# Order of the products in the up projections of a two-block transformer kernel, and the layout of their activation tile

## What is computed

```python
def swiglu(h, w_in, w_out):
    a, g = jnp.split(h @ w_in, 2, axis=-1)
    return (jax.nn.silu(a) * g) @ w_out
...
mlp = jnp.einsum('bsf,fd->bsd', jnp.square(jax.nn.relu(jnp.einsum('bsd,df->bsf', x, w_up[i]))), w_down[i])
gate = jax.nn.sigmoid((jnp.einsum('bsd,de->bse', x, w_ple_gate[i]) + b_ple_gate[i]).astype(jnp.float32)).astype(x.dtype)
```

## Time and profile before

| | |
|---|---|
| median of the three runs | 2022.68 us |
| lowest and highest run | 2021.26, 2022.79 us |
| span of the profiled execution | 2020.7 us |
| PE busy | 1988.9 us, 98% of the span |
| DVE, ACT busy | 1322.7 us, 857.5 us |
| mean granted TensorE clock | 0.997 |
| moved by DMA | 319.19 MB |

### The profile page before, as it was taken

One profiled execution on the slowest core, in us unless ns is written; L12 is line 12 of the kernel. 1 busy time (PEld: TensorE's weight loads), 2 busy tenths in 40 slices (PEclk: granted clock), 3 DMA queues, 4 the chain that ended last, 5 costly groups with the idle time before them and its releaser, 6 DMA issues.

```text
span 2020.7 us, 25508 instructions
## 1 busy us (share of the span) xinstructions
PE 1988.9 (98%) x10263; PEld 1654.0 (82%) x10263; DVE 1322.7 (65%) x1642; ACT 857.5 (42%) x1007; POOL 68.4 (3%) x121
## 2 busy tenths in 40 slices
PE   8999999999999999999999999999999999999998
PEld 5878778778888888877778888899888888988887
DVE  5886979556555354576776565766866577678565
ACT  5332332224322222446665554554544356445442
POOL 0000000010111000000000000000000000000000
PEclk9999999999999999999999999999999999999999
DMA  9544444252554343332137555545655554546552
GB/s 357 184 151 136 144 148 145 84 167 74 172 155 158 104 151 126 102 113 84 53 103 219 168 177 177 188 165 170 216 194 193 176 172 162 196 157 218 189 190 81
DMA packets 250759, 319.19 MB, mean 158 GB/s; under 512 B 10113, under 2 KB 166066, under 8 KB 250130
## 3 DMA queue, kind: packets, MB, share of 16 engines
q1 hardware_dynamic: 235152, 262.77, 40.2%
q0 software_dynamic: 14416, 53.14, 7.8%
q10 hardware_dynamic: 1074, 1.66, 0.2%
HBM read 316.48 MB, written 1.05 MB: 157 GB/s over the span
## 4 chain that ended last, share of the span: by engine, by line
PE 86%; DVE 6%; ACT 2%; DVEq 2%; DMA 1%; issue 1%; ACTq 1%; SPq 0%
PE ps L2326 14%; PE ps L2327 14%; PE ps L2321 8%; PE ps L2881 6%; PE ps L3142 6%; PE ps L2340 5%; PE ps L2336 5%; PE ps L2337 5%; PE ps L2798 3%; PE ps L2269 3%; PE ps L3145 3%; PE ps L2406 2%; PE ps L2887 2%; PE ps L2891 2%; PE ps L2888 2%; PE ps L2801 2%
## 5 line engine op out<-in xcount | busy, mean ns | idle before, releaser
L1241 DVE TENSOR_TENSOR w_lo<-raw,w_hi 128x2048 fp32r<-128x2048 f32 (+1 forms) x244 | 553.0, 2271 | 239.1 <-ACT w_hi L609 238.3
L609 ACT ACTIVATE w_hi<-raw 128x2048 fp32r<-128x2048 f32 (+1 forms) x244 | 462.0, 1897 | 254.3 <-PE ps L2321 149.6
L2326 PE MATMUL ps<-w_hi,big_hi 128*128 128x512 f32 x760 | 298.8, 393 | 0.9 <-DVE big_lo L1739 0.7
L2327 PE MATMUL ps<-w_hi,big_lo 128*128 128x512 f32 x760 | 296.2, 390 | 0.0
L2336 PE MATMUL ps<-hT_hi,w_hi 128*128 128x512 f32 (+1 forms) x512 | 192.4, 380 | 1.9 <-issue 1.0
L2337 PE MATMUL ps<-hT_lo,w_hi 128*128 128x512 f32 (+1 forms) x512 | 190.3, 376 | 0.0
L2326 PE MATMUL ps<-w_hi,hT_hi 128*128 128x512 f32 x416 | 167.7, 403 | 4.6 <-DVE hT_lo L1246 4.6
L2326 PEld LDWEIGHTS ps<-w_hi,big_hi 128*128 128x128 f32 x760 | 142.8, 188 | 30.4 <-issue 1.0
L2327 PEld LDWEIGHTS ps<-w_hi,big_lo 128*128 128x128 f32 x760 | 142.9, 188 | 28.9 <-issue 0.5
L2327 PE MATMUL ps<-w_hi,hT_lo 128*128 128x512 f32 x416 | 163.2, 392 | 0.0
L3142 PE MATMUL ps<-h_both,w_hi 128*128 128x512 f32 x512 | 128.0, 392 | 0.0
(11 more groups left out here) (314 smaller groups left out, 3027.4 us busy)
## 6 DMA issues: line engine op xcount, KB each, us to landing
raw<-ffn_w_in SPq DMA_DIRECT2D x88, 512.0 KB, 5.1
raw<-w_in SPq DMA_DIRECT2D x80, 512.0 KB, 4.6
raw<-w_up SPq DMA_DIRECT2D x64, 512.0 KB, 4.7
raw<-w_down SPq DMA_DIRECT2D x64, 512.0 KB, 4.5
raw<-ret_w_in SPq DMA_DIRECT2D x48, 512.0 KB, 5.4
front<-ada_w POOLq DMA_DIRECT2D x24, 1024.0 KB, 5.5
raw<-ffn_w_out SPq DMA_DIRECT2D x40, 512.0 KB, 4.5
raw<-ada_w POOLq DMA_DIRECT2D x64, 256.0 KB, 4.3
```

The costliest lines, as they stand in the source:

```text
L609: act.activation(SPLIT_HI[PAIR_OF[u]][:, 0:m], raw[:, RAW_OF[u], 0:m], ACT.Copy).then_inc(sem["hi_ready"], 1)
L1241: op(SPLIT_LO[PAIR_OF[u]][:, 0:m], raw[:, RAW_OF[u], 0:m], SPLIT_HI[PAIR_OF[u]][:, 0:m].bitcast(F32), ALU.subtract).then_inc(sem["lo_ready ...
L2326: pe.matmul(out, x[0][:, t * P:(t + 1) * P], w, start=start, stop=False)
L2327: pe.matmul(out, x[1][:, t * P:(t + 1) * P], w, start=False, stop=False)
```

## The change

The tile's axes are exchanged, so that the high and low columns of one k-tile lie side by side. The short products of a half no longer follow its long ones: those of half 0 stand one by one ahead of the long ones of half 1, and those of half 1 ahead of the long ones of half 0 of the next unit. The last half of each group of up units has its short ones in a run, as before. `used` of a unit moves to the last short product of its half 1, which now lies within the next unit, unless it is the group's last. The waits (`up_read`, `hi_ready`, `lo_ready`) stand where they stood, at the head of a unit and behind its first 8 long products. The lists of ACT, DVE, SP and POOL are not touched. Groups are units 2, 3 to 7, 8 to 11, 12 to 15 and 16 to 21 in the first block (`ups1`), and U0 to U3, four times two, and U12 to U15 in each layer (`ups`).

```diff
-        h2_both = sb("h2_both", [P, 2, KD, 256], F32R, hT_at)
-        h2_hi, h2_lo = (h2_both[:, j, :, :] for j in range(2))
+        h2_both = sb("h2_both", [P, KD, 2, 256], F32R, hT_at)
+        h2_hi, h2_lo = (h2_both[:, :, j, :] for j in range(2))
...
+                def up_low(n, j, k):
+                    out, js = up_out(n, j)
+                    w = SPLIT_LO[PAIR_OF[start_of[f"U{n}"]]].rearrange("p (k n) -> p k n", k=KD)
+                    return pe.matmul(out[:, 0, :], w[:, k, js], h2(k)[0], start=False, stop=(k == KD - 1))
+
+                def ups(first, last):
+
+                    for n in range(first, last):
+                        if n >= 2:
+                            pe.wait_ge(sem["up_read"], 20 + 16 * l + n - 1)
+                        w = unit(f"U{n}", 0, KD)
+                        out, js = up_out(n, 0)
                         for k in range(KD):
-                            pe.matmul(out, w[0][:, k, js], h2_both[:, :, k, :], start=(k == 0), stop=False)
+                            if n > first:
+                                m = up_low(n - 1, 1, k)
+                            pe.matmul(out, w[0][:, k, js], h2_both[:, k, :, :], start=(k == 0), stop=False)
+                        if n > first:
+                            used(m)
                         lows(w)
+                        out, js = up_out(n, 1)
                         for k in range(KD):
-                            i = pe.matmul(out[:, 0, :], w[1][:, k, js], h2(k)[0], start=False, stop=(k == KD - 1))
-                    used(i)
+                            up_low(n, 0, k)
+                            pe.matmul(out, w[0][:, k, js], h2_both[:, k, :, :], start=(k == 0), stop=False)
+                    for k in range(KD):
+                        m = up_low(last - 1, 1, k)
+                    used(m)
...
-                up(0)
-                up(1)
-                for g in range(5):
-                    up(2 * g + 2)
-                    up(2 * g + 3)
+                ups(0, 4)
+                down(0)
+                for g in range(1, 5):
+                    ups(2 * g + 2, 2 * g + 4)
                     down(g)
-                for n in range(12, 16):
-                    up(n)
+                ups(12, 16)
                 down(5)
```

More of the change, by code:

```diff
@@ L2787, in up1_rows, with up1_out, up1_low, ups1 @@
                 return m
[L2789 to L2796, removed]
-                    for k in range(KD):
-                        pe.matmul(out, w[0][:, k, js], h2_both[:, :, k, :], start=(k == 0), stop=False)
+            def up1_out(i, j):
+                return ps[:, UP_PAIR[(i + 1) % 2] + j, :].rearrange("p (a n) -> p a n", a=2), slice(j * P, (j + 1) * P)
+            def up1_low(i, j, k):
+                out, js = up1_out(i, j)
+                w = SPLIT_LO[PAIR_OF[FIRST_AT[f"f{i}"]]].rearrange("p (k n) -> p k n", k=KD)
+                return pe.matmul(out[:, 0, :], w[:, k, js], h2(k)[0], start=False, stop=(k == KD - 1))
+            def ups1(first, last):
+                for i in range(first, last):
+                    if i >= 4:
+                        pe.wait_ge(sem["up_read"], i - 3)
+                    elif i == 3:
+                        pe.wait_ge(sem["hid_lo"], 22 + 2)
+                    w = unit(f"f{i}", KD)
+                    out, js = up1_out(i, 0)
+                    for k in range(KD):
+                        if i > first:
+                            m = up1_low(i - 1, 1, k)
+                        pe.matmul(out, w[0][:, k, js], h2_both[:, k, :, :], start=(k == 0), stop=False)
+                    if i > first:
+                        used(m)
                     lows(f"f{i}")
+                    out, js = up1_out(i, 1)
                     for k in range(KD):
-                        m = pe.matmul(out[:, 0, :], w[1][:, k, js], h2(k)[0], start=False, stop=(k == KD - 1))
+                        up1_low(i, 0, k)
+                        pe.matmul(out, w[0][:, k, js], h2_both[:, k, :, :], start=(k == 0), stop=False)
+                for k in range(KD):
+                    m = up1_low(last - 1, 1, k)
                 used(m)
@@ L2824, in _ @@
             pe.wait_ge(sem["x_ready"], 12)
-            up1(2)
+            ups1(2, 3)
             for i in range(2):
@@ L2831, in _ @@
             gate_row(4)
-            up1(3)
-            for i in range(4, 8):
-                up1(i)
+            ups1(3, 8)
             pe.wait_ge(sem["rg_read"], 4)
             down1(0)
-            for i in range(8, 12):
-                up1(i)
+            ups1(8, 12)
             down1(1)
-            for i in range(12, 16):
-                up1(i)
+            ups1(12, 16)
             down1(2)
-            for i in range(16, 22):
-                up1(i)
+            ups1(16, 22)
             down1(3)
@@ L3132, in layer, with up_out @@
                     used(tile_rows(bank(4 + c), 1, w, h2, k0, 4, k0 == 0, k0 == 4))
[L3134 to L3140, removed]
-                        for k in range(KD):
-                            pe.matmul(out, w[0][:, k, js], h2_both[:, :, k, :], start=(k == 0), stop=False)
+                def up_out(n, j):
+                    return ps[:, UP_PAIR[n % 2] + j, :].rearrange("p (a n) -> p a n", a=2), slice(j * P, (j + 1) * P)
+                def up_low(n, j, k):
+                    out, js = up_out(n, j)
+                    w = SPLIT_LO[PAIR_OF[start_of[f"U{n}"]]].rearrange("p (k n) -> p k n", k=KD)
+                    return pe.matmul(out[:, 0, :], w[:, k, js], h2(k)[0], start=False, stop=(k == KD - 1))
+                def ups(first, last):
[4 more added lines that the diff above has]
+                        out, js = up_out(n, 0)
+                        for k in range(KD):
+                            if n > first:
+                                m = up_low(n - 1, 1, k)
+                            pe.matmul(out, w[0][:, k, js], h2_both[:, k, :, :], start=(k == 0), stop=False)
+                        if n > first:
+                            used(m)
                         lows(w)
+                        out, js = up_out(n, 1)
                         for k in range(KD):
-                            i = pe.matmul(out[:, 0, :], w[1][:, k, js], h2(k)[0], start=False, stop=(k == KD - 1))
-                    used(i)
+                            up_low(n, 0, k)
+                            pe.matmul(out, w[0][:, k, js], h2_both[:, k, :, :], start=(k == 0), stop=False)
+                    for k in range(KD):
+                        m = up_low(last - 1, 1, k)
+                    used(m)
                 def hid(k):
```

## The result

The changed kernel takes **2026.52 us** (median of 14 runs, 2025.11 to 2027.29); the kernel before, run beside it, 2022.36 us (14 runs, 2021.26 to 2022.79). The ratio is 1.0021, with an interval of [1.0013, 1.0028] that lies wholly above 1: slower by 0.2%, some 4 us. The time lies above the stated range, which ended at 2025.6. The profiled execution has a span of 2024.6 us, 3.9 more than before, at the same mean granted clock of 0.997.

What follows compares the result with a forecast made beforehand. PE's own back-to-back products, busy 98% of the span, were taken as the bound. Shorts taken apart, -4.15 us, and holes at the layer starts, +1.85, gave -2.3: 2022.7 to 2020.4 us, range 2017.6 to 2025.6.

Steps and rivals of the forecast that it cites:

- the price of the pair: Up units on PE: a single short and a long together cost 342 ns, 114 + 228, against 349.2 today.
- short products singly: Up units on PE: 87 runs of eight shorts taken apart, 72 of them counting, for -4.15 us.
- upper bound: Pair on PE: a short within a run, 120, and a long right behind one, 234, together 354 ns.
- lower bound: Pair on PE: a short right behind a long, 114, and an undisturbed long, 226.5, together 340.5 ns.
- The first rival: Pairs on PE: every switch costs, 348 to 354 ns a pair, kernel slower at 2024.0 to 2027.7 us; 25%.
- The layout: Activation tile: 512 adjacent columns for the long products' moving operand, put at 0.
- The holes: Start of each layer: PE waits 1.2 us ahead of U3 for DVE's add of U1; together +1.85 us.
- The second rival: Layer starts: the waits at U3 don't hold PE, 86 runs count, -5.0, 2017.7 us; 10%.
- The steady units: Units after the layer starts: `used` moves back, 1.4 us of slack left, 15 waits cost nothing.
- The third rival: Steady units: DVE reads too late everywhere, 15 holes of about 0.9, +13, 2034 us; 5%.
- The loads hidden all along: Pairs on PE: the pair stays at 349.2 ns and only holes of 2.1 remain, 2024.8 us; 7%.
- Queues, and all else: Queues and waits: same instructions, no transfer; splits and SP's loads some 1.7 us later, needed over 16 us after.

Runs made afterwards that it cites:

- experiment 11: Changed kernel with the gate operations later, each group's first half keeping its run of eight shorts, then single shorts at a distance of two; 2025.54 us.
- experiment 2: Kernel before with only the new tile layout, old order of products; 2022.1 us, ratio 1.0.
- experiment 1: Changed kernel with the tile's old layout, so only the order of products is new; 2026.28 us, ratio 1.0019.
- experiment 3: Changed kernel with DVE's two gate operations behind the add of U1 instead of ahead of it; 2024.53 us, ratio 1.0011.
- experiment 12: Changed kernel, gate operations later, distance eight kept; each group starts with thirteen longs, eight shorts in a run, three longs, then singles; 2020.98 us, ratio 0.9992.
- experiment 5: Kernel before, old layout, with a unit's sixteen long products first and then its sixteen short ones; 2021.13 us, ratio 0.9996.
- experiment 9: Changed kernel with the gate operations later, each group's first half keeping its run of eight shorts, then single shorts at distance three; 2021.35 us, ratio 0.9993.

## Why the prediction was wrong

**The step that failed is the price of the pair**, in the part on short products singly: 342 ns, taken as 114 + 228 between bounds of 340.5 and 354. It was 353.3, next to the upper bound. Mostly it was the long's term: behind a single short it took 232, 241 and 235 in turn, 236 in the mean, not 228; the short took 117 in the mean, not 114. With the text's own formula 72 runs x 8 x (353.3 - 349.2) = +2.4 us stands where -4.15 stood. The nine runs of units 3 to 7 came out at 346.7, which takes 9 x 8 x 6.6 ns = 0.5 from it, so +1.9; the account has +2.0 without the layer starts. The reason given for 342, that the record of the first short is 278 ns long and those of the later ones 283, so that a single short leaves the next long alone, fell: in the alternation the shorts' records are 277, 281, 284 and 278 ns long, one after the other, so the longer ones come although no short follows another. Neither bound was a steady price. 114 and 234 are the first steps behind a switch, and the next switches come before those have run out; the prediction took them for prices that add up. The 340 of the lower bound did occur, at distance two, for the first pair of a group and no longer (experiment 11). By the working's own terms a pair of 351 comes to some 2025.9 us and not to the 2025.6 at which its range ended; the measured time lies above either.

**Right, by its step.** The first rival, "every switch costs", gave 348 to 354 a pair and 2024.0 to 2027.7 us; the measured 353.3 and 2026.52 lie in it. It should have had more than 25%: its row was without exception, and the case against it was an argument, mainly from durations. But its mechanism holds only in part, and that its sum of 354 came so close is partly luck: the terms were 120 and 234, the rows have 117 and 236; the price depends on how the alternation is entered; and with runs of two the switches are more than before and the round is cheaper (2.785 against 2.793).

**The layout** was put at 0 and is 0 in the old order (experiment 2); in the new order only units 3 to 7 differ, by 0.47 us, with the other rhythm (experiment 1).

**The holes** were predicted at U3 of each layer, released by L2224, +1.85 us in all, at a pair of 342 and 2.2 at 354. They are there, and the two layer starts cost +2.06 with their pairs, 1.64 of it the holes (experiment 3). U3's first product starts 16.70 us behind U0's first, as forecast (16.73); the idle stretch ahead of it is 0.6 us, not 1.2. The forty pairs ahead of it, each 11.3 ns dearer than forecast, brought PE there 0.45 us later; the rest is a matter of counting, since the profile counts from the recorded end of the last long, 0.40 us behind its start, and the working from the step of some 0.23. The last eight shorts stand behind it, as the text had it. The second rival (no hole) is out.

**The steady units** have no wait on `up_read`: PE's waits on L2224 are those two. The third rival is out.

**The loads hidden all along** (349.2 in either order, 2024.8 us) is out as well, by 353.3 and 346.7 in one trace. The Trainium skill ("TensorE: Matmul & The Clock Gate", "Step-by-step: what each phase is for") has the next product's weights load while the present product runs, and the prediction drew from it that a pair costs the same in either order. The trace agrees that they overlap, the load being recorded 1 to 5 ns behind the start of the product ahead. It doesn't agree with the equal price: the same loads and products took 353.3 or 346.7 ns a pair.

**Queues, and all else:** outside the 17 stretches the span changed by 3.9 - 4.0 = -0.1 us.

## What to carry to other kernels

Where PE's products stand back to back, the order of products of two sizes was worth up to two per cent of their time here (346.7 to 353.3 a pair, with the 349.2 of runs of eight between them). The steps seen at a switch give bounds and not the price of an alternation: put a stretch of it on the chip before building the order on it. Look at more than one group, since the price can be one of two steady rhythms, fixed by the way into the alternation. And when the reader of a bank loses slack through a new order, look at the place where that engine's list is full: moving two independent operations behind the read took back 1.6 of the 4.0 us.

## What was not expected of the hardware

An alternation of products of 512 and 256 columns, each with its own load, has **two steady rhythms**: 346.7 ns a pair (117 and 230), and a cycle of three pairs of 346, 358 and 356 (mean 353.3). Which of them it is went with the steps of PE ahead of the first short, not with the distance of the two parts (346.7 at three and eight, 353.3 at two, six and eight), with banks (at distance three a group has pairs within a bank and across two, all at 346.7) or with the granted clock, which was 1.00 in both. With the new layout both rhythms occur; the old layout was measured in one kernel of this kind, and there only 353.3 came, so whether it can hold 346.7 is not shown. 346.7 is also what a settled long and a settled short in their own runs sum to, 226.7 + 120; no alternation in these runs was steadily below it. With it the order of the change would have been right in its aim but small: all 17 stretches together are 1.7 us shorter (experiment 12), 0.08% of the kernel, and by the medians experiments 5, 9 and 12 can't be told from the kernel before.
